# A hybrid recurrent and convolution encoder block: products on array quarters, first weights loaded earlier, a transform stage spread over tiles

## The chip, the cores and the metric

The kernel runs on one core of one Trainium2 chip. Its time is the device time of one execution in microseconds (us); the median of several runs is given. The profiled execution is a run of its own.

## The reference

One encoder block over 2048 tokens of 1024 channels, float32. The first half of the block, in which the change lies, computes this (RMSNorm, GeLU and the expert layer behind it are as usual):

```python
proj = rmsnorm(x) @ w_in                      # 1024 -> 2560: lru_x | lru_gate | v | x1 | x2, 512 each
xc = dwconv4(lru_x)                           # per direction d, heads of 64 channels:
r, i = sigmoid(xc @ wr + br), sigmoid(xc @ wi + bi)   # block diagonal, 8 blocks of 64 x 64
log_a = -8 * r * softplus(-lam);  a = exp(log_a)
h = scan(a, sqrt(1 - a * a) * (i * xc))       # forwards, and with other weights backwards
y_lru = (h_forward + h_backward) * gelu(lru_gate)
z = sin(f1 * (feats @ w1 + b1)); z = sin(f2 * (z @ w2 + b2))
filters = (z @ w3) * decay                    # 2 orders x 2 directions x 512 channels x 2048 positions
k = fft(filters / sum(abs(filters)))
y_hy = x2 * longconv(x1 * longconv(v, k1), k2)        # by FFT; v, x1, x2 through dwconv3 first
x = x + concat(rmsnorm(y_lru), rmsnorm(y_hy)) @ w_out
x = x + moe(rmsnorm(x))                       # top-1 of 4 groups, top-2 of 8 experts
```

## The kernel before

The program is a chain of stages. Within each, the five engines run programs of their own that are written out by hand and held together by semaphores; each engine and each queue works strictly in its written order. Between stages all engines meet, and SP clears the semaphores of the next one.

**Norm and filters** (`norm_and_filters`, L110). x is normalised and transposed. The filter network gives `zzd`, a pair of halves of 64 rows, the unused ones zero. The long filters are then made in 32 steps j (position j modulo 32). `generate` (L229) is one product for each of two orders o: stationary 128 x 128 out of `zzd`, moving `w3`, 512 channels. The stationary operand is block diagonal, forward filter and backward filter. VectorE multiplies the result by the decay (L374), ScalarE takes the magnitude (L303), GpSimd sums it (L200), `transform` (L243) is the first stage of the FFT of an earlier step, ScalarE empties its bank (L309) and SP stores it. On TensorE the order is generate(j), transform(j - 2). SP loads each decay tile (256 KB) four steps ahead. ScalarE and VectorE also split the normalised x into a high and a low part (L319, L355). At the end the sum goes through a product with ones (L255) and sixteen small ones (L259); with these the skip is scaled and added to filter row 0 (L379, L382), and the last transform follows.

**Projections** (`project_and_lru`, L396). The 2560 columns of `w_in` are 20 tiles of 128. A tile is 4 chunks of 512 tokens x 8 blocks of rows x 3 products of high and low parts, 96 passes (L521). SP loads its weights two tiles ahead (L457), ScalarE rounds them (L583), VectorE subtracts (L698). `TILES` gives the order: for each c of 0 to 3 the tiles v, x1, x2 of 128 channels (the last x2 after x of the RG-LRU), then x and g of the RG-LRU in turn. A tile of v, x1 or x2 is convolved by VectorE (L704, L706) and transposed (L543). For v the transposes go on into `spread` (L552), the first FFT stage of the signal: for each c 4 pieces of two products with 64 rows each, ScalarE empties them (L616) and stores them. `turn` does all four pieces at once, ahead of the transposes of the following x1 tile.

**RG-LRU**, inside the same stage, for each c: `gate` (L534) computes four gates (two kinds, two directions) of 4 chunks each, a block-diagonal 128 x 128 stationary operand made of two heads. ScalarE applies the sigmoids (L591). `decay` is Exp, Tanh and Sqrt (L634 to L637). VectorE: `weigh` (L725), `lru_input` (L729, L731), the scans (L735), `add_directions` (L739), the next convolution, the weight subtraction, and `gate_result` (L744). The gates of c + 1 may write T, the sigmoids' output, only when `gate_result` of c is done.

**Convolution** (`conv`, L798) is sent to the same engines behind the stage before. Of each block, `k_product` (L933) and `z_product` (L944) use column halves of the array and `inverse` (L957) row halves. GpSimd makes one difference per block (L1050), and for block 0 a one-row copy (L1054). VectorE runs the last backward scan, the last addition and the last gate product between the blocks 0, 3 and 6.

## Time and profile before

| | us |
|---|---|
| median of 3 runs | 2301.02 (2298.18 to 2305.28) |
| profiled execution | 2303.28 |
| its span | 2301.5 |
| TensorE busy | 2068.6 (90%) |
| VectorE busy | 1221.4 (53%) |
| ScalarE busy | 1115.4 (48%) |
| GpSimd busy | 345.9 (15%) |

The span runs from the first to the last instruction, and busy times are shares of it. PE is a product on TensorE, PEld a weight load, DVE is VectorE, ACT ScalarE, POOL GpSimd, SPq the queue of SP. A timeline row gives start, length, engine, line, operation, output and input by the program's names, how many instructions are merged, and in brackets the idle time ahead with what ended it. A merged row of products is as long as from the first start to the last end, and the ends of pipelined products overlap the next start. Every fp32 product appears as two passes; those of the projections (fp32r) as one.

### The profile page before, as it was taken

How to read it: one execution, taken by the hardware profiler on the slowest of the kernel's cores; microseconds unless marked ns; L12 is line 12 of the kernel's file. 1: busy time of each engine (PE TensorE's matmuls, PEld its weight loads, DVE VectorE, ACT ScalarE, POOL GpSimd, SP SyncE). 2: the span in 40 equal slices, each digit the busy share in tenths (PEclk: the TensorE clock that was granted, in tenths of full speed). 3: DMA queues.
4: the chain of work that ended last, by engine and by line, in shares of the span. 5: the costliest groups of instructions: out<-in, count | busy, mean ns of one | idle time of the engine just before them, and what ended most of it. 6: DMA issues, size and time to landing. Idle time of an engine off the chain costs nothing. (4 is left out here: it accounts for less than half of the span.)

```text
span 2301.5 us, 30650 instructions
## 1 busy us (share of the span) xinstructions
PE 2068.6 (90%) x9069; PEld 1500.0 (65%) x9070; DVE 1221.4 (53%) x1111; ACT 1115.4 (48%) x1315; POOL 345.9 (15%) x309
## 2 busy tenths in 40 slices
PE   3996999999999997878999669999999999999990
PEld 1654787786666421226878558888788788888870
DVE  7552322223666654663444475466868655664643
ACT  6762222225555532342333145466867765665643
POOL 0560000000000230220000011212111121221120
PEclk9997999999999999998999769999999999999995
DMA  5461213213111699757542356787999987886858
GB/s 190 157 226 62 64 55 92 73 37 94 39 38 38 244 341 348 273 192 249 178 165 96 128 193 196 249 275 252 374 310 375 374 293 222 297 284 207 291 145 313
DMA packets 239629, 462.08 MB, mean 201 GB/s; under 512 B 24897, under 2 KB 87461, under 8 KB 235174
## 3 DMA queue, kind: packets, MB, share of 16 engines
q1 hardware_dynamic: 201798, 375.17, 45.6%
q0 software_dynamic: 14400, 52.44, 9.5%
q10 hardware_dynamic: 23360, 33.56, 4.5%
q8 instruction: 42, 0.69, 0.1%
q14 instruction: 29, 0.23, 0.0%
HBM read 346.79 MB, written 114.29 MB: 200 GB/s over the span
## 5 line engine op out<-in xcount | busy, mean ns | idle before, releaser
L1762 PE MATMUL p<-wh_hi,x_hi 128*128 128x512 f32 x768 | 309.0, 402 | 1.7 <-DVE x_lo L1876 0.6
L1762 PE MATMUL p<-wh_hi,x_lo 128*128 128x512 f32 x768 | 304.4, 396 | 0.0
L1762 PE MATMUL p<-wh_lo,x_hi 128*128 128x512 f32 x768 | 304.2, 396 | 0.0
L1888 DVE TENSOR_TENSOR wh_lo<-w_raw,wh_hi 128x2048 fp32r<-128x2048 f32 x128 | 284.8, 2286 | 27.6 <-ACT wh_hi L1849 27.6
L521 PE MATMUL ps<-h_hi,wp_hi 128*128 128x512 f32 x640 | 257.7, 403 | 15.3 <-DVE wp_lo L698 15.3
L521 PE MATMUL ps<-h_lo,wp_hi 128*128 128x512 f32 x640 | 254.6, 398 | 0.0
L521 PE MATMUL ps<-h_hi,wp_lo 128*128 128x512 f32 x640 | 254.3, 397 | 0.0
L1849 ACT ACTIVATE wh_hi<-w_raw 128x2048 fp32r<-128x2048 f32 x128 | 234.8, 1924 | 0.4 <-DMA w_raw<-in_exp_w_dram 0.4
L1050 POOL TENSOR_TENSOR arena<-arena 128x512 f32<-128x512 f32 x32 | 56.9, 1778 | 762.4 <-DVE arena L1066 762.4
L1762 PEld LDWEIGHTS p<-wh_hi,x_hi 128*128 128x128 f32 x768 | 144.9, 189 | 35.6 <-issue 1.7
L1762 PEld LDWEIGHTS p<-wh_hi,x_lo 128*128 128x128 f32 x768 | 145.0, 189 | 35.2
L1762 PEld LDWEIGHTS p<-wh_lo,x_hi 128*128 128x128 f32 x768 | 145.0, 189 | 32.8
L1762 PE MATMUL pyy<-wy_hi,a_hi 128*128 x392 | 159.9, 408 | 5.9 <-ACT yb L1833 4.7
L1762 PE MATMUL pyy<-wy_hi,a_lo 128*128 x392 | 155.8, 398 | 0.0
L1762 PE MATMUL pyy<-wy_lo,a_hi 128*128 x392 | 155.6, 397 | 0.0
L521 PEld LDWEIGHTS ps<-h_hi,wp_hi 128*128 128x128 f32 x640 | 121.4, 190 | 46.5 <-DVE wp_lo L698 16.9
L1888 DVE TENSOR_TENSOR wy_lo<-w_raw,wy_hi 128x2048 fp32r<-128x2048 f32 x64 | 144.2, 2286 | 8.8 <-ACT wy_hi L1849 8.8
L1903 DVE TENSOR_TENSOR a<-p,s 128x512 f32<-128x512 f32 x48 | 33.2, 691 | 214.6 <-ACT s L1862 214.6
L521 PEld LDWEIGHTS ps<-h_lo,wp_hi 128*128 128x128 f32 x640 | 121.3, 190 | 29.5 <-issue 1.0
L521 PEld LDWEIGHTS ps<-h_hi,wp_lo 128*128 128x128 f32 x640 | 121.2, 189 | 29.5
L589 ACT ACTIVATE hraw<-ps 128x512 f32<-128x512 f32 x48 | 28.7, 599 | 221.0 <-PE ps L521 221.0
L1849 ACT ACTIVATE wy_hi<-w_raw 128x2048 fp32r<-128x2048 f32 x64 | 120.8, 1923 | 25.0 <-DMA w_raw<-in_exp_w_dram 21.5
(300 smaller groups left out, 3537.0 us busy)
## 6 DMA issues: line engine op xcount, KB each, us to landing
w_raw<-in_exp_w_dram SPq DMA_DIRECT2D x512, 256.0 KB, 5.9
w_raw<-in_exp_w_dram SPq DMA_DIRECT2D x128, 512.0 KB, 10.7
scratch_KA<-work SPq DMA_DIRECT2D x32, 512.0 KB, 3.0
scratch_SI<-arena SPq DMA_DIRECT2D x32, 512.0 KB, 3.4
kin<-scratch_KA SPq DMA_DIRECT2D x21, 512.0 KB, 6.1
arena<-scratch_SA SPq DMA_DIRECT2D x21, 512.0 KB, 5.1
wp_raw<-in_w_in_dram SPq DMA_DIRECT2D x20, 512.0 KB, 3.8
h_raw<-in_x_dram ACTq DMA_DIRECT2D x4, 2048.0 KB, 20.2
```

The costliest lines, as they stand in the source:

```text
L521: last = pe.matmul(out, w[:, s, k, :], h, start=(k == 0 and i == 0), stop=(k == KC - 1 and i == 2))
L589: ins = act.activation(out[:, 512 * n:512 * (n + 1)], pj[n], func)
L1050: dif = pool.tensor_tensor(yr[:, n % 2, :], by_r[:, n % 2, 0, :], by_i[:, n % 2, 1, :], ALU.subtract)
L1762: mm = pe.matmul(acc[:, :], x[:, k, :], w, start=(k == 0 and i == 0), stop=(k == n - 1 and i == 2))
L1849: act.activation(place, raw[:, j:j + 2, :], ACT.Copy).then_inc(rounded, 1)
L1888: dve.tensor_tensor(lo, raw[:, j:j + 2, :], hi.bitcast(F32), ALU.subtract).then_inc(lowered, 1)
L1903: dve.tensor_tensor(a[:, :], p3[:, :], s1[:, :], ALU.mult).then_inc(a_ready, 1)
```

## The change

`generate` and the gates of c = 1 to 3 no longer use one block-diagonal product of 128 rows and 128 columns but two of 64 x 64, each on its own quarter of the array, and the second order (or the backward direction) uses the two other quarters. So that one's results lie with their partition halves exchanged. The tables `fa_filter` and `decay` get a second, rolled copy for the second order (decay: 512 KB a step), `zzd` becomes `zz` of half the size. In the RG-LRU the backward direction of c = 1 to 3 lives in exchanged halves: GpSimd issues copies that exchange the parameters once, `xc` after each convolution (into the buffer of `xraw`), and the backward scan's result before the addition. `gate` of c = 0 stays.

The first two weight tiles are loaded by SP in the filter stage, behind the last `generate`, into the place of `zz`, and the loads at the start of the projections go. The skip waits for the norm product alone. `spread` is called for one piece behind each chunk of the projection of the tile after x1 (j = 2, 5, 8, 11), and ScalarE empties and stores it there. `gate_result` runs in four chunks, each waiting for its chunk of G; from c = 1 on, `add_directions` stands behind the next convolution and the weight subtraction. `early_loads` of the convolution waits for the last exchanged product instead of the last convolution.

```diff
@@ -118,21 +118,25 @@
     with ExitStack() as ctx:
         sb = lambda name, shape, dt=F32: ctx.enter_context(nc.sbuf_tensor(name, shape, dt))
         sem = PhaseSemaphores(nc, ctx)
+        marks["w_at"] = -(-nc.sbuf_base // 32) * 32
+        ka1, acc_flat = sb("ka1", [P, 2 * CH]), sb("acc", [P, 2 * CH])
+        marks["w_raw_at"] = -(-nc.sbuf_base // 32) * 32
+        zz = sb("zz", [P, SEQ])
+        w_first = nc.alloc_sbuf_tensor_at("w_first", [P, 2, KC, P], F32, offset=marks["w_raw_at"])
...
-        dec = sb("dec", [P, 4, CH])
-        ka1, acc_flat = sb("ka1", [P, 2 * CH]), sb("acc", [P, 2 * CH])
...
             for j in range(N2):
                 if j >= 4:
...
                 if j >= 5:
                     store(j - 5)
             sp.wait_ge(k_ready, N2 - 2)
-            sp.dma_start(skip, dram["hy_skip"]).then_inc(skip_in, 16)
+            for o in range(2):
+                sp.dma_start(skip[o], dram["hy_skip"][:, o, :]).then_inc(skip_in, 16)
+            sp.wait_ge(kgen, N2)
+            w_v = dram["w_in"].rearrange("o (k p) n -> p (o k) n", p=P)
+            for j, column in enumerate((1024, 1536)):
+                sp.dma_start(w_first[:, j], w_v[:, :, column:column + P]).then_inc(w_first_in, 16)
             for i in range(N2 - 5, N2):
                 store(i)
+            sp.wait_ge(w_first_in, 32)
             for s in range(3):
                 sp.wait_ge(kst_out[s], 16 * len(range(s, N2, 3)))
...
             pe.wait_ge(mlp_sin, 3)
-            view = zzd.rearrange("p h (q l) -> p l h q", l=N2)
+            view = zz.rearrange("p (q l) -> p l q", l=N2)
 
             def generate(j):
                 if j >= 2:
                     pe.wait_ge(k_ready, j - 1)
                 for o in range(2):
-                    last = pe.matmul(pk[j % 2][:, o, :], view[:, j], w3[:, o, :], start=True, stop=True)
+                    for h in range(2):
+                        rows, out = slice(R * h, R * h + R), slice(R * (h ^ o), R * (h ^ o) + R)
+                        last = pe.matmul(pk[j % 2][out, o, :], view[rows, j], w3[rows, o, :], start=True, stop=True)
...
 
             generate(0)
@@ -252,12 +265,13 @@
             pe.wait_ge(k_ready, N2)
             pe.wait_ge(summed, N2 + 2)
             for o in range(2):
-                pe.matmul(pk[0][:, o, :], ones[:, :], acc[:, o, :], start=True, stop=True)
+                last = pe.matmul(pk[0][:, o, :], ones[:, :], acc[:, o, :], start=True, stop=True)
+            last.then_inc(norm_mm, 1)
             for o in range(2):
                 for c in range(CT):
                     place = (o * CT + c) * 2
                     last = pe.matmul(pk[1][:, 0, place:place + 2], acc[:, o, c * P:(c + 1) * P], ones[:, 0:2], start=True, stop=True)
-            last.then_inc(norm_mm, 1)
+            last.then_inc(sums_mm, 1)
             transform(N2 - 1)
...
                     low_part(j // 2 - 2)
             dve.wait_ge(norm_mm, 1)
-            dve.wait_ge(skip_in, 16)
-            dve.scalar_tensor_tensor(out=skip, in0=pk[0][0:1, :, :], scalar=EPS, in1=skip, op0=ALU.add, op1=ALU.mult).then_inc(norm_ready, 1)
-            dve.wait_ge(norm_ready, 1)
+            dve.wait_ge(skip_in, 32)
+            for o in range(2):
+                dve.scalar_tensor_tensor(out=skip[o], in0=pk[0][R * o:R * o + 1, o, :], scalar=EPS, in1=skip[o], op0=ALU.add, op1=ALU.mult).then_inc(norm_ready, 1)
+            dve.wait_ge(norm_ready, 2)
             dve.wait_ge(abs_ready, 1)
-            dve.tensor_tensor(kt0[0:1, :, :], kt0[0:1, :, :], skip, ALU.add).then_inc(k0_ready, 1)
+            for o in range(2):
+                first = kt0[R * o:R * o + 1, o, :]
+                dve.tensor_tensor(first, first, skip[o], ALU.add).then_inc(k0_ready, 1)
             for i in range(NT - 2, NT):
                 low_part(i)
+            dve.wait_ge(sums_mm, 1)
...
         w_lo, w_raw = in_place(nc, ctx, "wp", [P, 2, KC, P])
+        raw_tile = lambda j: (marks["w_first"] if j < 2 else w_raw)[:, j % 2]
...
             rows = [("lru_conv_w", Q_CONV_W), ("lru_conv_b", Q_CONV_B), ("lru_br_f", 5), ("lru_bi_f", 6),
                     ("lru_br_b", 7), ("lru_bi_b", 8), ("lru_lambda_f", 9), ("lru_lambda_b", 10),
                     ("hy_conv_w", Q_HW), ("hy_conv_b", Q_HB), ("grp_norm_lru_g", Q_GA), ("grp_norm_hy_g", Q_GA + 1)]
@@ -506,6 +525,18 @@
             pool.memset(prow[:, :], 0.0)
             pool.memset(WG[:, :, :], 0.0).then_inc(zeroed, 1)
 
+            def exchange(out, a, done):
+                for h in range(2):
+                    pool.dma_start(out[halves[h]], a[halves[1 - h]]).then_inc(done, 16)
+
+            pool.wait_ge(lam_ready, 1)
+            exchange(PT_swapped, PT, pt_swapped)
+            for c in range(1, CT):
+                pool.wait_ge(xc_ready, c + 1)
+                exchange(xc_swapped, xc, xc_exchanged)
+                pool.wait_ge(scanned, 2 * c + 2)
+                exchange(I[1], T[1], exchanged)
+
...
+                    if j < 12 and j % 3 == 2:
+                        spread(j // 3, n)
                     if j == 0 and n == 0:
...
+            def gate_quarters(c):
+                pe.wait_ge(xc_ready, c + 1)
+                pe.wait_ge(wg_in, 16 * 8 * (c + 1))
+                for kind in range(2):
+                    for n in range(NCHUNK):
+                        u = kind * NCHUNK + n
+                        b = 2 * (u % 2)
+                        pe.wait_ge(evac, after(gate_place[c] + u // 2 - 1, b + 1))
+                        for d in range(2):
+                            for h in range(2):
+                                rows, out = halves[h], halves[h ^ d]
+                                last = pe.matmul(pj[b + d][out, :], WG[rows, 2 * d + kind, R * h:R * h + R], xc[rows, n * 512:(n + 1) * 512],
+                                                 start=True, stop=True)
+                            last.then_inc(mm_done, 1)
+
             def transposes(s):
 
...
-            def spread(c):
-
-                for b in range(4):
-                    pe.wait_ge(tr_evac, c * PER_C + SPREAD + (0 if b < 2 else 2 * b - 2))
-                    for g in range(2):
-                        h = slice(g * HALF, g * HALF + HALF)
-                        pe.matmul(tp[2 * b % 4 + g], fs[h, :], tst[h, 4 * b:4 * b + 4, :], start=True, stop=True).then_inc(tr_done, 1)
-
-            def turn(s):
-                if s % 3 == 1:
-                    spread(s // 3)
-                transposes(s)
+            def spread(c, b):
+
+                pe.wait_ge(tr_evac, c * PER_C + SPREAD + (0 if b < 2 else 2 * b - 2))
+                for g in range(2):
+                    h = slice(g * HALF, g * HALF + HALF)
+                    pe.matmul(tp[2 * b % 4 + g], fs[h, :], tst[h, 4 * b:4 * b + 4, :], start=True, stop=True).then_inc(tr_done, 1)
...
             def high(j):
-                act.wait_ge(w_in[j % 2], 16 * (j // 2) + 16)
-                act.activation(w_hi[:, j % 2], w_raw[:, j % 2], ACT.Copy).then_inc(w_high, 1)
+                at_least(act, w_in[j % 2], 16 * (j // 2))
+                act.activation(w_hi[:, j % 2], raw_tile(j), ACT.Copy).then_inc(w_high, 1)
...
-                    high(j + 1)
-                evacuate(f, out, func, chunks=range(2, 4))
+                for n in range(NCHUNK):
+                    if n == 2 and 1 <= j < len(TILES) - 1:
+                        high(j + 1)
+                    evacuate(f, out, func, chunks=range(n, n + 1))
+                    if j < 12 and j % 3 == 2:
+                        evacuate_spread(j // 3, n)
 
             def evacuate_turned(s):
-                if s % 3 == 1:
-                    act.wait_ge(tr_done, s // 3 * PER_C + SPREAD + 8)
-                else:
+                if s % 3 != 1:
...
+                act.wait_ge(tr_evac, first + 2 * b + 2)
+                act.dma_start(dram["SA"][0][:, 8 * b:8 * b + 8, c * P:c * P + P],
+                              spread_out[:, b % 2].rearrange("p l g n -> p (l g) n")).then_inc(sa_out[b % 2], 16)
 
             def decay(c, d):
-                act.wait_ge(evac, after(gate_place[c] + 2 * d))
+                act.wait_ge(evac, after(gate_place[c] + (1 if c else 2 * d)))
                 if d:
                     act.wait_ge(scanned, 2 * c + 1)
                 elif c:
                     act.wait_ge(y_out, 16 * c)
                 else:
...
+            def sigmoid_quarters(c):
+                for kind in range(2):
+                    for n in range(NCHUNK):
+                        u = kind * NCHUNK + n
+                        for d in range(2):
+                            bank = 2 * (u % 2) + d
+                            act.wait_ge(mm_done, after(gate_place[c] + u // 2, bank))
+                            act.activation((T, I)[kind][d][:, 512 * n:512 * (n + 1)], pj[bank], ACT.Sigmoid,
+                                           bias=col_of((Q_BR, Q_BI)[kind][d], c, d)).then_inc(evac, 1)
 
...
+                    if c == 1:
+                        act.wait_ge(pt_swapped, 32)
+                    sigmoid_quarters(c)
                 decay(c, 0)
...
-                    act.wait_ge(xc_ready, c + 1)
+                    if c:
+                        act.wait_ge(weighed, c)
+                    else:
...
             def weigh(c, d):
-                dve.wait_ge(evac, after(gate_place[c] + 2 * d + 1))
-                step(dve.tensor_tensor(I[d], I[d], xc, ALU.mult))
+                dve.wait_ge(evac, after(gate_place[c] + (3 if c else 2 * d + 1)))
+                if c and d:
+                    dve.wait_ge(xc_exchanged, 32 * c)
+                    dve.tensor_tensor(I[d], I[d], xc_swapped, ALU.mult).then_inc(weighed, 1)
+                    dve.wait_ge(weighed, c)
+                else:
+                    step(dve.tensor_tensor(I[d], I[d], xc, ALU.mult))
 
...
             def add_directions(c):
                 dve.wait_ge(scanned, 2 * c + 2)
-                step(dve.tensor_tensor(T[0], T[0], T[1], ALU.add))
+                if c:
+                    dve.wait_ge(exchanged, 32 * c)
+                step(dve.tensor_tensor(T[0], T[0], I[1] if c else T[1], ALU.add))
 
             def gate_result(c):
                 by_row = lambda a: a.rearrange("p (n q) -> p n q", n=HALF)
-                dve.wait_ge(evac, after(place["g", c]))
-                dve.tensor_tensor(Q.rearrange("p (q n) -> p n q", n=HALF), by_row(T[0]), by_row(G), ALU.mult).then_inc(y_ready, 1)
+                for n in range(NCHUNK):
+                    rows = slice(n * HALF // NCHUNK, (n + 1) * HALF // NCHUNK)
+                    dve.wait_ge(evac, after(place["g", c], n))
+                    last = dve.tensor_tensor(Q.rearrange("p (q n) -> p n q", n=HALF)[:, rows], by_row(T[0])[:, rows], by_row(G)[:, rows], ALU.mult)
+                last.then_inc(y_ready, 1)
 
...
                 lru_scan(1)
-                add_directions(c)
+                if c == 0:
+                    add_directions(c)
                 lru_conv(c + 1)
                 low(TILES.index(("g", c)) + 1)
+                if c:
+                    add_directions(c)
                 gate_result(c)
...
         def early_loads(sp):
-            sp.wait_ge(marks["xc_ready"], CT)
+            sp.wait_ge(marks["weighed"], CT - 1)
             sp.dma_start(kin[0], pair_rows("KA", 0)).then_inc(kin_in[0], 16)
...
-    out = dict(fa_filter=F, fa_signal=np.concatenate([F[:HALF], F[:HALF]]), inv_a=IA,
+    out = dict(fa_filter=np.stack([F, np.roll(F, HALF, 0)], 1), fa_signal=np.concatenate([F[:HALF], F[:HALF]]), inv_a=IA,
                fwd_b=full.reshape(N2, P, P).transpose(1, 0, 2), inv_b=inv.reshape(PAIRS, P, 2, P).transpose(1, 0, 2, 3),
-               feats=feats, decay=decay, ident=np.eye(P))
+               feats=feats, decay=np.stack([decay, np.roll(decay, HALF, 0)], 2), ident=np.eye(P))
     return {k: np.ascontiguousarray(v, dtype=f) for k, v in out.items()}
 
```

## Rows read from the trace of the kernel before

**Rows 1.** Busy time by stage: length, engines, TensorE clock, DMA share, GB/s.
```profile
74.40:175.70 101.30, 101.30 (x238) 57.26 (x237) 53.76 (x44) 72.33 (x75) 72.96 (x31) 1.00 0.66 219
204.30:549.80 345.50, 334.68 (x1489) 263.58 (x1490) 96.39 (x82) 83.18 (x142) 0.00 (x0) 0.98 0.23 65
549.80:769.80 220.00, 214.82 (x819) 151.92 (x820) 139.74 (x57) 137.89 (x145) 0.00 (x0) 1.00 0.15 41
```

**Rows 2.** Timeline of TensorE in the filter loop.
```profile
124.18 1.88 PE L229 MATMUL fk<-w,zzd 128*128 128x512 f32 x4
...
127.62 1.88 PE L229 MATMUL fk<-w,zzd 128*128 128x512 f32 x4
```

**Rows 3.** Timeline of TensorE in the convolution blocks, on array halves.
```profile
954.29 1.99 PE L957 MATMUL ps<-arena,inv_b 64*128 64x512 f32 x8
...
959.79 1.99 PE L957 MATMUL ps<-arena,inv_b 64*128 64x512 f32 x8
```

**Rows 4.** DMA queue in the filter loop (74.4 to 175.7): packets, MB, share.
```profile
q1 hardware_dynamic: 11668, 22.08, 66.2%
```

**Rows 5.** DMA queue at the convolution's start (770 to 800).
```profile
q1 hardware_dynamic: 3926, 11.31, 97.4%
```

**Rows 6.** Timeline of TensorE at the end of the filters.
```profile
180.90 1.84 PE L259 MATMUL fk<-ones,acc 128*128 128x2 f32 x16
```

**Rows 7.** Timeline of VectorE where the projection stage starts.
```profile
197.77 0.06 DVE L691 MEMSET xraw<- 128x2 f32 x1 [9.94 <-PEq L88]
```

**Rows 8.** Timeline of ScalarE, the same place.
```profile
201.98 1.06 ACT L583 ACTIVATE wp_hi<-wp_raw 128x1024 fp32r<-128x1024 f32 x1 [11.85 <-DMA wp_raw<-in_w_in_dram]
```

**Rows 9.** Timeline of TensorE: last passes of projection tiles 1, 2, 3, 8 and 9.
```profile
250.77 0.40 PE L521 MATMUL ps<-h_hi,wp_lo 128*128 128x512 f32 x1
...
274.97 0.40 PE L521 MATMUL ps<-h_hi,wp_lo 128*128 128x512 f32 x1
...
306.54 0.40 PE L521 MATMUL ps<-h_hi,wp_lo 128*128 128x512 f32 x1
...
434.91 0.40 PE L521 MATMUL ps<-h_hi,wp_lo 128*128 128x512 f32 x1
...
468.06 0.40 PE L521 MATMUL ps<-h_hi,wp_lo 128*128 128x512 f32 x1
```

**Rows 10.** Timeline of TensorE, gates of c = 1.
```profile
610.45 3.59 PE L534 MATMUL ps<-hc,WG 128*128 128x512 f32 x8
615.77 10.57 PE L534 MATMUL ps<-hc,WG 128*128 128x512 f32 x24 [1.72 <-ACT hraw L591]
```

**Rows 11.** Timeline of VectorE in the RG-LRU.
```profile
611.28 3.72 DVE L744 TENSOR_TENSOR tst<-hraw,spread 128x2048 f32<-128x2048 f32 x1 [0.72 <-ACT spread L589]
...
662.81 7.12 DVE L706 SCALAR_TENSOR_TENSOR hc<-xraw,PT,hc 128x2048 f32<-128x2048 f32 x3
```

**Rows 12.** Timeline of ScalarE, sigmoids of c = 1.
```profile
615.03 2.42 ACT L591 ACTIVATE hraw<-ps,PT 128x512 f32<-128x512 f32 x4 [2.19 <-DVE tst L744]
...
627.08 1.28 ACT L634 ACT_TABLE_LOAD   x1
```

**Rows 13.** Timeline of VectorE at the convolution's start: the last scan.
```profile
780.30 4.41 DVE L735 TENSOR_TENSOR_SCAN hraw<-tst,hc 128x2048 f32<-128x2048 f32 x1
```

**Rows 14.** Timeline of GpSimd, the same place.
```profile
778.33 1.77 POOL L1050 TENSOR_TENSOR arena<-arena 128x512 f32<-128x512 f32 x1 [579.97 <-DVE arena L1066]
780.16 4.95 POOL L1054 COPY arena<-arena 1x512 f32<-1x512 f32 x1
```

**Rows 15.** Timeline of TensorE, the same place.
```profile
786.31 2.94 PE L957 MATMUL ps<-arena,inv_b 64*128 64x512 f32 x8
```

**Rows 16.** Single lines of GpSimd: durations in ns, least, median, most.
```profile
L1054 POOL COPY arena<-arena x2: 687/2819/4951, 780.2 to 941.6; 1x512 f32<-1x512 f32 x2
...
L1715 POOL DMA_INDIRECT xg<-scratch_H,curidx x50: 993/1003/2869, 1349.4 to 2231.5; - x50
...
L1728 POOL DMA_INDIRECT scratch_X<-yb,curspot x50: 1586/1606/1623, 1368.1 to 2249.0; - x50
```

More of the change, by code:

```diff
@@ L134, in norm_and_filters @@
         ka, acc, kt0 = [kst[:, 3], split(ka1)], split(acc_flat), split(gain)
-        skip = dec[0:1, 0:2, :]
+        skip = [dec[R * o:R * o + 1, 0, o, :] for o in range(2)]
         pair = lambda name: ctx.enter_context(nc.psum_tensor(name, [P, 2, CH], F32))
@@ L242, in transform @@
                 for o in range(2):
-                    last = pe.matmul(pa[i % 2][:, o, :], fa[:, :], tile(j)[:, o, :], start=True, stop=True)
+                    last = pe.matmul(pa[i % 2][:, o, :], fa[:, o, :], tile(j)[:, o, :], start=True, stop=True)
                 last.then_inc(fa_done, 1)
@@ L441, in project_and_lru @@
         steps = sem("p_steps")
+        pt_swapped, xc_exchanged, weighed, exchanged = (sem(n, 0) for n in ("pt_swapped", "xc_exchanged", "weighed", "exchanged"))
+        halves = [slice(R * h, R * h + R) for h in range(2)]
         w_v = dram["w_in"].rearrange("o (k p) n -> p (o k) n", p=P)
@@ L573, in _ @@
                 if TILES[j] in GATED:
-                    for g in range(4):
-                        gate(GATED[TILES[j]], g)
+                    gate_quarters(GATED[TILES[j]])
         @block.scalar
```

75 lines of the change are left out of this document (33 added, 42 removed).

## The prediction, made before the changed kernel was run

> **What bounds the kernel now.** I read the page first, then the busy time by stage, then TensorE's timeline in each stage that the diff touches, and last what the other engines do where TensorE waits. The stages [rows 1] show TensorE busy for all 101.3 us of the filter loop, for 334.7 of the 345.5 us of the first twelve projections, and for 214.8 of the 220.0 us in which the RG-LRU follows. There the reader is to see that nothing else comes near: ScalarE has 72.3, 83.2 and 137.9 us in the same stretches. So in these stages a change is worth what it takes off TensorE's own sequence. What it takes off another engine is worth only what TensorE waits for that engine. The share of the copies is 0.66 in the filter loop, which matters below.
>
> **Filter loop.** One step is one `generate` (two fp32 products, each run as two passes over 512 columns) and one `transform` (the same). `generate` starts at 124.18 and again at 127.62 us [rows 2]: a step is 3.44 us, and its eight passes take 0.43 us each with no gap. The change splits each product of `generate` into two with 64 rows and 64 columns. That makes eight passes in place of four, on four quarters of the array. The trace before has no quarters. It has halves: in the convolution blocks [rows 3] eight passes on halves (x8) take 1.99 us or less, so two run at once, and a block of 24 passes that changes twice between row halves and column halves repeats every 5.50 us (954.29 to 959.79). Twelve slots of 0.43 us would be 5.16, so two changes of array shape cost 0.34 us. From these rows `generate` is bounded by 0.86 us (four quarters at once), 1.72 (two at once, as the halves) and 3.44 (one at a time). I take 0.86: halves by row and halves by column each overlap fully, and the four quarters of one `generate` are distinct in both. TensorE's step is then 1.72 + 0.86 + 0.34 = 2.92 us.
>
> The next limits, over the 29.5 steps of the stretch [rows 1]: ScalarE 72.33 / 29.5 = 2.45 us, GpSimd 2.47, VectorE 1.82, all below 2.92. The copies are not. The decay table is now loaded twice as wide, so a step moves 512 + 512 KB = 1.05 MB instead of 0.79. The filter loop moved 22.08 MB in 101.3 us at a share of 66.2% [rows 4], which is 329 GB/s for full engines: 3.19 us a step. The stretch with the heaviest traffic shows 11.31 MB in 30 us at 97.4% [rows 5], or 387 GB/s: 2.71 us. The new table has rows of twice the length, nearer to the second. Copies and TensorE compete for the bound and do not mesh perfectly, so I take 3.1 us a step. The saving is 0.34 x 29 = 9.9 us (bounds 2.93: 14.8; 3.44: none).
>
> The Trainium skill (TensorEngine Tiling (Array Packing), Restrictions and Gotchas) says that different row tiles cannot access the same PSUM bank simultaneously. Here the two row halves of one `generate` product do write one bank, on different partitions; the halves in this trace always wrote different banks, so no row bears on it. By the rule only two quarters could run at once, or fewer; these are the second and third rivals below.
>
> **Filter tail.** The VectorE step that adds the skip to filter row 0 now waits only for the four norm passes, not for the sixteen small products behind them, which take 1.84 us [rows 6]. Its two instructions become four of half the length; I charge 0.2 us for the extra starts. Saving 1.6 us (bounds 0.5 and 1.8). The three memsets taken from VectorE at the start hid behind the wait for parameters: nothing.
>
> **First weights.** VectorE enters the projection stage at 197.77 us [rows 7], ScalarE rounds the first weights at 201.98 after a wait for their copy [rows 8], and TensorE follows by rounding and subtracting. Loaded during the filters, they let ScalarE start at once: 4.2 us, less 0.2 for four more semaphores that are cleared in between: 4.0 (bounds 3 and 4.5). What is moved: two 512 KB copies are issued ahead of the last five filter stores on SP's queue, and the first waits for the last `generate`. Store 27 goes out some 3.5 us later, and ScalarE's evacuation 30 waits for it; only the last transform is behind that, which has to wait for the norm anyway. The parameter rows are now issued first by SP and gain 1 us.
>
> **Transform stage spread over projection tiles.** From the last pass of one projection to that of the next is 24.20 us without a spread (250.77 to 274.97), 31.57 with the first (274.97 to 306.54) and 33.15 with the third (434.91 to 468.06), which also met a slow clock [rows 9]; the second is like the first and the fourth like the third. The four cost 2 x 7.4 + 2 x 8.95 = 32.7 us. Of that 16 passes in pairs are 3.44 us each time; the rest is waiting for ScalarE to empty the banks and for stores to land. After the change one piece (four passes in pairs, 0.86 us, and two changes of shape, 0.34) stands behind each quarter of a projection, 5.6 us apart, while ScalarE has 5 us free. So 4 x 1.2 = 4.8 us for each c, and 0.5 for the transposes, whose third bank still waits for the last piece: 4 x 5.3 = 21.2 us. Saving 11.5 us (bounds 8, if every change of shape costs double, and 14). Nothing is idle long enough in it for the clock to fall.
>
> **RG-LRU gates, c = 1 to 3.** Now the first eight passes start at 610.45, TensorE waits 1.72 us for ScalarE, and 24 more start at 615.77 and take 10.0 us to the next projection [rows 10]: 15.3 us for each c. ScalarE starts its sigmoids at 615.03, when VectorE has done the gate product (611.28, 3.72 us) [rows 11, 12]. Three quarters of that product can now run before the last piece of G is there, but behind the weight rounding, which ends 0.72 us before 611.28 [rows 11]: it ends at about 614.4, 0.6 us sooner. (From c = 1 the addition of the directions stands ahead of it in place of ahead of the convolution, 2.3 us that only change places.) Then the first four sigmoids, whose banks are full, take 2.42 us [rows 12], 0.6 each, so a unit of quarters costs ScalarE 1.2 us and TensorE, from bank free to result, about 1.3 (0.86, one weight load, the drain). With four banks these alternate at about 1.28 us a unit. The next projection needs the first bank of unit 6: 8.7 us after the first sigmoid, against 10.7 now. Saving 0.6 + 2.0 = 2.6, three times 7.7 us (bounds 3 and 10). ScalarE's own chain, which now leaves the sigmoids 12.0 us after their start (627.08), gains about as much, so the next tile's banks are not late.
>
> Added: two exchange copies of 1 MB for each c between partition halves, issued by GpSimd, which is idle here; the copies' share in this stage is 0.15 [rows 1]. The first has 10 us of cover (it is needed after the sigmoids). The second is issued at the end of the backward scan and needed behind the next convolution, 7.1 us for its last three taps alone [rows 11], and one weight rounding: nothing, as long as it lands within that.
>
> **Start of the convolution.** Here a wait is added with something behind it. GpSimd's program is in order: its last exchange waits for the last backward scan (780.30 + 4.41 us [rows 13]), and behind it stands the first difference of the convolution, which ran before that scan, with its one-row copy ending at 785.1 [rows 14]. TensorE's first inverse product started at 786.31 [rows 15] and needs it. After: scan end 784.7, two copies issued (no row for this kind; bounds nothing and the 1.6 us of GpSimd's scatter; I take the gather's 1.0, being the plainer of the two [rows 16]), then 1.77 for the difference and, without the scan beside it, 0.69 for the copy (4.95 beside it; both in [rows 16]): 789.3. TensorE is 3.1 us late and has idled into the slow clock, another 1.2: a loss of 4.3 us (bounds 1.5 and 8). The products of the next blocks leave no slack to win it back.
>
> **Sum.** 9.9 + 1.6 + 4.0 + 11.5 + 7.7 - 4.3 = 30.4 us. The profiled execution took 2303.3 us (span 2301.5); it becomes 2272.9. The median of the runs, 2301.0, is 2.3 lower: 2271.
>
> **Rivals.**
> First, the filter loop is bound by its copies: at 329 GB/s or less with the doubled table, a step stays at 3.3 to 3.44 us. For it: at equal efficiency to now the step is already 3.19. Against: longer rows. The filter part falls to 0 to 4: about 2279.
> Second, two quarters at a time: `generate` keeps 1.72 us and gains two changes of shape, a step of 3.78, which loses 0.34 x 29 = 9.9 us where 9.9 was gained; the gates, at 1.72 + 0.45 a unit, win only the 0.6 and a little. Left: 1.6 + 4.0 + 11.5 + 1 - 4.3 - 9.9 = 3.9 us, 2297, no change that can be told.
> Third, the other side: quarters run one at a time, because two row tiles hold one bank. `generate` is 3.44 us and a step 5.50: 60 us lost in the filters. A unit of gates is 3.44, eight are 27.5 against 15.3: 37 lost. Less 12.8 from the rest: 2301 + 84 = 2385. The point from which it decides: the rest of the change saves 12.8 us, which 29 steps eat up when four quarter products cost 1.8 us, 0.45 each; all at once they cost 0.21, in pairs 0.43.
> Fourth, the second exchange lands late. For it: GpSimd's one-row copy was held to 4.95 us beside a scan, so issuing beside VectorE may be slow too. Against: 7.1 us and more of cover, and idle copy engines. Price: 1 to 3 us for c = 1 and 2, and a longer hold of GpSimd at the end: about 2277.
>
> **Chances.** Forecast 0.60; first 0.14; fourth 0.10; second 0.09; third 0.05; something unseen 0.02. What a measurement of this kernel can tell from no change is about 0.3%, 7 us. Faster 0.86, same 0.07, slower 0.07. The forecast's own bounds (sums of the likely ends of its parts) are 2260 to 2281; with the first and fourth rival, and a part of the second, the range is 2258 to 2289.
>
> **What would show it.** Right: `generate`'s eight passes start within 0.5 us of one another and the filter step is near 3.1 us with the copies' share above 0.9; ScalarE's first rounding directly behind the stage's start; a projection tile with pieces near 29 us from last pass to last pass; next projection 8.7 us after the first sigmoid; GpSimd's first difference after the last backward scan and the first inverse product some 3 us later in its stage. Wrong: a step of 3.8 or 5.5 us, a wait of the addition of directions for the exchange, or a wait of the projections for banks that ScalarE now empties later.

## The result and the profile after

The changed kernel takes 2273.43 us (median of 4 runs, 2272.07 to 2274.30) and the kernel before 2303.15 (4 runs, 2298.18 to 2306.78): a ratio of 0.9868, 95% interval 0.9848 to 0.9889, so 1.3% faster. Forecast were 2271 us with a range of 2258 to 2289. The profiled execution took 2273.04 us with a span of 2271.3 us, 30.2 less than before, and the sum had 30.4. The total is right to 0.2 us, but its terms are not: one gain was sized 4.1 us too small, one did not appear, and the loss came out twice as large and by another mechanism.

The stages again, cut at the same events as [rows 1]: filter loop, first projections, RG-LRU (the prediction calls the second stretch twelve projections; it holds thirteen tiles, the first x of the RG-LRU among them. Columns as there; PE is TensorE, the last three are clock, DMA share, GB/s):
```profile
72.90:163.60 90.70, 90.65 (x356) 30.95 (x356) 52.59 (x44) 74.01 (x77) 86.03 (x31) 1.00 0.92 326
187.10:520.90 333.80, 333.80 (x1490) 259.99 (x1491) 96.16 (x82) 82.83 (x142) 1.32 (x2) 0.99 0.24 67
520.90:732.40 211.50, 200.76 (x914) 139.55 (x914) 139.19 (x66) 135.51 (x145) 6.16 (x10) 0.98 0.26 68
```
TensorE fills the filter loop as before, and now the projections too, where [rows 1] left 10.8 us idle. In the third stage it has 10.7 us of idle time, where [rows 1] has 5.2.

TensorE's timeline in the filter loop (start, duration to the last end, engine, line, names, shapes, count), which answers to [rows 2]:
```profile
118.73 1.02 PE L256 MATMUL fp<-work,fa 128*128 128x512 f32 x2
119.68 1.16 PE L242 MATMUL fk<-w,zz 64*64 64x512 f32 x8
120.78 1.98 PE L256 MATMUL fp<-work,fa 128*128 128x512 f32 x4
122.69 0.73 PE L242 MATMUL fk<-w,zz 64*64 64x512 f32 x4
```
`generate` starts at 119.68 and again at 122.69, a step of 3.01 us. Its eight quarter passes are over, and the transform has begun, 1.10 us after the first began. Two at a time they alone would need 1.72. The first four start within 20 ns of one another, the other four 0.54 us later. So four quarters ran at once, although the two row halves of a product write one PSUM bank on different partitions. Here the rule that the prediction cites (the Trainium skill, TensorEngine Tiling (Array Packing), Restrictions and Gotchas) did not hold the passes back. The rivals built on it, 2297 and 2385 us, are out.

The start of the convolution, first TensorE's timeline (in brackets: idle time before, and what ended it), then GpSimd's. They answer to [rows 14, 15]:
```profile
745.80 1.94 PE L997 MATMUL ps<-kin,fwd_b 128*64 128x512 f32 x8 [2.22 <-DMA fwd_b<-in_fwd_b_dram]
750.36 1.99 PE L1021 MATMUL ps<-arena,inv_b 64*128 64x512 f32 x8 [2.62 <-POOL arena L1118]
752.28 1.94 PE L1008 MATMUL ps<-arena,fwd_b 128*64 128x512 f32 x8
760.25 3.68 PE L997 MATMUL ps<-xraw,fwd_b 128*64 128x512 f32 x8 [6.03 <-DMA xraw<-scratch_KA]
763.86 2.94 PE L1021 MATMUL ps<-arena,inv_b 64*128 64x512 f32 x8
```
```profile
746.88 1.01 POOL L530 DMA_DIRECT2D hc<-hraw  x2 [52.69 <-DVE hraw L791]
747.91 1.28 POOL L1114 TENSOR_TENSOR arena<-arena 128x512 f32<-128x512 f32 x1
749.26 0.96 POOL L1118 COPY arena<-arena 1x512 f32<-1x512 f32 x1
```
GpSimd does what was foreseen: last scan, two issues of 0.5 us each, difference, one-row copy, and TensorE waits 2.62 us for it. Nothing foresaw the second wait. After one more product TensorE stands 6.03 us for the kernel block of block 3, the fourth one, and its passes then run at a granted clock of 0.50 (3.68 us for eight, 1.94 at 1.00 before the wait). From 747 to 777 us the queues show this:
```profile
q1 hardware_dynamic: 3356, 8.23, 78.6%
q0 software_dynamic: 160, 1.05, 14.9%
...
hc<-hraw POOLq DMA_DIRECT2D x2, 512.0 KB, 9.7
```
The 1.05 MB of the exchange take 14.9% of the sixteen engines for 30 us, 4.5 us of all of them. Before the change the loads filled this stretch (785 to 815 us there) to 97.1%. The load that TensorE waits for was issued long before the exchange and landed 22.7 us later. SP's timeline has its issue:
```profile
737.53 0.47 SPq L915 DMA_DIRECT2D xraw<-scratch_KA  x1
```
While the exchange's packets move (750.6 to 756.8 us) the loads get only 0.47 MB through. In the 3.5 us behind them it is 1.18 MB. The queues from 750.6 to 756.8 us:
```profile
q0 software_dynamic: 158, 1.05, 71.9%
q1 hardware_dynamic: 244, 0.47, 32.1%
```
From the last projection pass to the third inverse product, behind which the blocks repeat every 5.50 us, were 29.2 us and are 38.5.

### The profile page after: what moved, and what is told of

Same layout as the page of the kernel before. It is cut to its first block and busy times, and to the rows that moved or that the text cites. A ratio compares the mean times of both kernels' runs of the same rounds, so it can differ in the third digit from the quotient of the medians.

```text
span 2271.3 us, 31131 instructions
## 1 busy us (share of the span) xinstructions
PE 2038.0 (90%) x9293; PEld 1451.9 (64%) x9294; DVE 1216.1 (54%) x1123; ACT 1113.4 (49%) x1315; POOL 363.0 (16%) x323
## 3 DMA queue, kind: packets, MB, share of 16 engines
q0 software_dynamic: 15424, 58.78, 10.9%
## 5 line engine op out<-in xcount | busy, mean ns | idle before, releaser
L552 PEld LDWEIGHTS ps<-h_hi,wp_lo 128*128 128x128 f32 x640 | 120.8, 189 | 29.3
L1789 POOL COPY curspot<-spot 128x1 int32 x50 | 44.1, 882 | 526.7 <-ACT yb L1897 526.7
```

What stands on the lines that cost most here:

```text
L552: last = pe.matmul(out, w[:, s, k, :], h, start=(k == 0 and i == 0), stop=(k == KC - 1 and i == 2))
L1789: pool.tensor_copy(cur_spot[:, :], spot[:, ds(B, 1)]).then_inc(spot_ready, 1)
```

## The experiments

All kernels below ran in three sets, five rounds each. The kernel before had medians of 2301.99, 2304.18 and 2303.62 us in them. "The stretch" is the one just named. Differences from the control compare medians, also between sets.

### First set: the exchange at the start of the convolution

**control**, the changed kernel itself. 

> The changed kernel again, beside the others. Expected: 2273 us, the ratio to the kernel before between 0.985 and 0.989, and the same 38.5 us from the last projection pass to the first steady block of the convolution.

 Measured: 2274.13 us, ratio 0.9875 [0.9857, 0.9894], stretch 38.5 us.

**c3_full**, whole array for c = 3 (the early loads of the convolution wait for the last convolution again, as before the change):
```
-  for c in range(1, CT):   # GpSimd's exchanges
+  for c in QUARTERS:       # (1, 2)
...
-  gate_quarters(GATED[TILES[j]])
+  if GATED[TILES[j]] in QUARTERS: gate_quarters(...)
+  else: for g in range(4): gate(..., g)
```


> Only c = 3 goes back to gate products on the whole array, so the last exchange (2 transfers, 1 MB) is gone and the last sum is a plain addition. Theory (the last exchange costs the convolution its start: GpSimd waits for the last scan before its first subtraction, and the transfer takes the engines that bring the first kernel blocks): the stretch from the last projection pass to the steady block, 38.5 us now and 29.2 before the change, falls to about 30, the gates of c = 3 grow by 2.1 us, in all 6 us less, 2267. Rival (that stretch is long since TensorE starts it at the lower clock after a longer idle time, and the loads are late of themselves): it stays at 36 or more, and the run is 2273 to 2276.

 Measured: 2270.06 us, ratio 0.9862 [0.9842, 0.9882], 4.1 less than the control, with 31.4 us for the stretch. The stage before it is 1.9 us longer (546.9 against 545.0 us from the first projection pass to the last). The wait for the same kernel block in TensorE's timeline:
```profile
757.05 2.52 PE L1003 MATMUL ps<-xraw,fwd_b 128*64 128x512 f32 x8 [2.64 <-DMA xraw<-scratch_KA]
```
It is 2.64 us, not 6.03. The theory holds in its main part and the rival falls: 7.1 of the 9.3 us are the exchange's. The same kernel run again (c3_again, below) has 29.8 us for the stretch, so up to 8.7.

The traces also settle which half of the exchange costs. Here the block's load was issued 5.9 us behind the last projection pass and landed 16.4 us later; in the changed kernel it was issued 5.7 us behind and took 22.7. TensorE reaches this product 22.4 us behind the last projection pass in this run, 28.4 in the changed kernel. Without the late load the changed kernel, its wait for GpSimd included, would have been ready for it at 754.2 us, which is 22.4 too. So the 2.62 us of GpSimd stand in the shadow of the load and cost nothing of their own. c3_again agrees. There another load made the first inverse product 1.9 us later than here (17.7 and 15.9 us behind the last projection pass), and the third comes 1.6 us earlier all the same, since TensorE waits 0.45 us for the block, not 2.64, and keeps its clock:
```profile
752.54 2.40 PE L1027 MATMUL ps<-arena,inv_b 64*128 64x512 f32 x8
...
757.25 1.94 PE L1003 MATMUL ps<-xraw,fwd_b 128*64 128x512 f32 x8 [0.45 <-DMA xraw<-scratch_KA]
```

**gates_full**, `QUARTERS = ()`, no exchange at all. 

> All gates on the whole array, no exchange at all; the filters, the first weights, the spread stage and the gate product by chunks stay as changed. Theory: the gates part of the change gains about 7.4 us in c = 1 to 3 and gives back about 8 at the start of the convolution, so this run is at 2273 within 2 us. Rival (the start of the convolution has nothing to do with the exchanges): the gates' 7.4 us are lost and nothing comes back, 2281.

 Measured: 2276.47 us, ratio 0.9884 [0.9863, 0.9904], stretch 29.3 us. That is 1.5 us outside the expected 2273 within 2 us (2.3 above the control), and 4.5 us below the rival's 2281. The stage before is 549.8 us long, 4.8 more than the control's, and 9.2 us come back in the stretch. At the end of the first round of blocks 6.7 of them are left (120.8 us from the last projection pass, 127.5 in the control), so there this kernel is 1.9 us ahead. Yet its span is 2.5 us longer (2274.7 against 2272.2). The stages behind, which the edit does not touch, differ by several us from run to run, and one pair of traces carries no statement of this size about the total.

**exch_sp1**, the last exchange on SyncE's queue behind block 1's loads; GpSimd no longer issues it, and the early loads stay as changed:
```
+  def last_exchange():
+      sp.wait_ge(scanned, 2 * CT)
+      for h in range(2): sp.dma_start(I[1][halves[h]], T[1][halves[1 - h]]).then_inc(exchanged_last, 16)
...
+  if n == 1: marks["last_exchange"]()
```


> The last exchange is issued by SyncE, behind the loads of block 1 of the convolution, instead of by GpSimd ahead of its subtractions. If GpSimd's order in its queue is what costs (its first subtraction stood 2.6 us behind the scan), about 2.6 us come back and the late loads stay: 2271. If the traffic of the exchange is what costs (the wait on the first kernel blocks, 6.0 us), it is now queued behind those blocks and 5 to 8 us come back: 2266 to 2268. If the addition at block 3 now waits for the transfer on VectorE, some of it is lost again there: 2270 or more with a wait at the addition.

 Measured: 2272.33 us, ratio 0.9868 [0.9846, 0.9889]. TensorE's waits from 733 to 850 us in the changed kernel and then in this one (line waited, releaser: us in total, times, longest):
```profile
PE ps L997 <- DMA xraw<-scratch_KA: 6.8, 2, 6.0
PE ps L997 <- DMA kin<-scratch_KA: 3.2, 1, 3.2
PE ps L1021 <- POOL arena L1118: 2.6, 1, 2.6
```
```profile
PE ps L1010 <- DMA kin<-scratch_KA: 5.1, 2, 3.2
PE ps L1010 <- DMA xraw<-scratch_KA: 3.1, 2, 2.5
```
The wait for GpSimd's copy is gone and the long wait is 2.5 us. But a later block (`kin`) now waits 1.9 us more. The stretch is 31.6 us, as in c3_full, so the place of the early loads is not what costs. The next inverse product comes 2.3 us later than in c3_full: part of the loss has moved. None of the three forecasts fits as it was written. The start came back as in the second, the total did not, and the addition does not wait for the transfer. The total can't be told from the control's (2267.53 to 2275.04 us in single runs).

### Second set: what bounds the filter loop now

**half_decay**, which does not load the second order's half of the decay table and uses the first for both:
```
-  sp.dma_start(dec[:, j % 4], dram["decay"][:, j])
+  sp.dma_start(dec[:, j % 4, 0], dram["decay"][:, j, 0])
```


> The filter loop loads 256 KB of decay factors a step, not 512 KB; the other half is read from the first again, so the second kernel's halves get each other's factors (wrong values, same work on every engine). Theory (TensorE sets the step of 3.00 us, the copies only run close to it): the step stays at 3.00 and the run at 2273 to 2274. Rival (the copies set it, with 0.93 of the 16 engines taken): the step falls towards 2.8, times 30, and the run to 2268 or less.

 Measured: 2274.13 us, ratio 0.9869 [0.9854, 0.9885], a step of 3.00 us.

**paired**:
```
-  for j in range(2, N2):
-      generate(j)
-      transform(j - 2)
+  for j in range(2, N2, 2):
+      generate(j)
+      generate(j + 1)
+      for i in range(max(j - 3, 0), j - 1): transform(i)
```


> In the filter loop TensorE generates two columns and then transforms two, so it changes between quarters and full array once in two steps. Theory (a step of 3.00 is 2.57 us of passes and 0.43 us of two changes of shape): it falls to 2.79, times 30 this is 6.3 us, 2268. Rival 1 (the copies are next, since 0.93 of the engines at 3.00 us leaves a floor of 2.79): between 2.8 and 2.95, 2 to 6 us. Rival 2 (the changes cost nothing, and the 0.43 us is something else, such as the first pass's own fill): the step stays at 3.00, 2273.

 Measured: 2273.75 us, ratio 0.9861 [0.9844, 0.9879]. Twelve pairs in a row take 72.5 us: 3.02 us a step.

**paired_half**, both edits. 

> Both edits: pairs, and 256 KB of decay factors a step (the second kernel's factors are wrong, the work is the same). If the copies hold the pairs back, this is faster than the pairs alone: step 2.79 and 2267 or less. If TensorE or another engine holds them back, it equals the pairs alone.

 Measured: 2274.08 us, ratio 0.9865 [0.9849, 0.9880]; 2.91 us a step.

The same 70 us of the loop in the changed kernel, half_decay, paired and paired_half (columns as in [rows 1]):
```profile
84.00:154.00 70.00, 70.00 (x285) 23.72 (x282) 41.75 (x35) 57.10 (x59) 66.33 (x24) 1.00 0.99 355
```
```profile
84.00:154.00 70.00, 70.00 (x285) 23.74 (x281) 41.75 (x35) 57.02 (x59) 66.33 (x24) 1.00 0.81 264
```
```profile
84.00:154.00 70.00, 68.51 (x281) 25.20 (x280) 48.56 (x35) 56.32 (x60) 65.71 (x26) 1.00 0.99 353
```
```profile
84.00:154.00 70.00, 70.00 (x290) 25.68 (x289) 66.60 (x37) 58.78 (x61) 66.19 (x25) 1.00 0.80 272
```
In the changed kernel TensorE is busy throughout and the copies are at 0.99. A share of 0.99 alone would name the copies. Taking a quarter of the traffic away (0.99 to 0.81) leaves the step at 3.00, so TensorE holds it. Giving TensorE less to do also leaves it, and then TensorE idles for 1.5 us and VectorE waits for the copies, in its list of waits:
```profile
DVE work L389 <- DMA dec<-in_decay_dram: 19.1, 19, 1.6
```
Both bounds lie at 3.0 us. Each edit alone gains nothing, and both together gain 0.09 us a step, 2.7 us in the loop; VectorE is then busy for 66.60 of 70 us, and what holds it at 2.91 I have not taken apart. The total does not show the 2.7 us. In the profiled run the end of the filters (from the last transform of the loop to the last of all) is 13.9 us long, 11.1 in the changed kernel and 12.7 in its control, and its products run at the lower clock. My expectation took the 0.93 of the whole loop for the copies' share. In these 70 us it is 0.99, and a floor of 2.97 would have followed.

**c3_paired**, paired and c3_full together. 

> The pairs of the filter loop, and c = 3's gates on the full array (no last exchange). The two savings are in different stages and should add: 4.1 us of c = 3 (2270.1 against 2274.1 in the first set) and what the pairs alone give, so 2264 if they give 6.

 Measured: 2266.61 us (2265.44 to 2269.38), ratio 0.9837 [0.9823, 0.9850]: the fastest version, with an interval wholly below the control's. The 2264 expected with 6 us from the pairs was missed.

### Third set: the other parts undone, and the exchange later

**spread_old**, the transform stage in one piece per c behind its tile, as before:
```
-                    if j < 12 and j % 3 == 2:
-                        spread(j // 3, n)
...
+            def turn(s):
+                if s % 3 == 1:
+                    spread(s // 3)
+                transposes(s)
```


> Only the transform stage goes back to one piece per c behind a projection tile. Theory (each c loses the idle time of TensorE between the spread passes, which the projection passes now fill): 11.9 us over the twelve projections, as between the two traces, so 2286 against the control's 2274. Rival (part of the 11.9 us is not this edit's: the projections start in another phase of the clock and of the loads): 5 to 8 us, 2279 to 2282.

 Measured: 2285.75 us, ratio 0.9927 [0.9914, 0.9939], 11.6 above the control. From the first projection pass to the last it takes 555.9 us against 545.0. The theory holds. (At the thirteenth tile 10.3 us of the 10.9 are there.)

**weights_old**, the first two weight tiles loaded in the projection stage. 

> Only the first two weight tiles are loaded at the start of the projection stage again, as before. Theory: the first projection then stands about 19 us behind the last transform of the filters and not 15.4, so 3.7 us later and 2278. Rival (the small transfers ahead of the projection, or the split of the weights on ScalarE and VectorE, hold the first pass anyway): under 1 us, 2274 to 2275.

 Measured: 2279.44 us, ratio 0.9893 [0.9880, 0.9906], 5.3 above the control. From the last transform to the first projection pass are 16.7 us against 12.9. ScalarE's first rounding in this kernel, then in the changed one, where [rows 8] has a wait of 11.85:
```profile
188.48 1.06 ACT L622 ACTIVATE wp_hi<-wp_raw 128x1024 fp32r<-128x1024 f32 x1 [12.23 <-DMA wp_raw<-in_w_in_dram]
```
```profile
184.63 2.00 ACT L625 ACTIVATE wp_hi<-w_first 128x1024 fp32r<-128x1024 f32 x2 [8.40 <-PEq L88]
```
The theory holds at 3.8 us; the other 1.5 us of the total no landmark shows. (The numbers of "19 and 15.4" in the expectation counted to another event; their difference is what was tested.)

**exch_sp3**, as exch_sp1 with `if n == 3`, the addition at block 5 and the gate product at block 7. 

> The last exchange is issued by SyncE behind the loads of block 3 of the convolution, its addition stands at block 5 and the last gate product at block 7. Theory (the start of the convolution is bound by transfers, so the megabyte costs its own 4.5 us of the 16 engines wherever it is put there): the first blocks are as early as without the exchange (31 us behind the last projection pass, not 38.5), about 4 us are lost over the next blocks, 2271 to 2272, as with the exchange behind block 1. Rival (it only had to leave the first loads alone): nothing is lost later, 2267 to 2268.

 Measured: 2270.48 us, ratio 0.9855 [0.9840, 0.9870]. The stretch is 31.6 us. From the last projection pass to the end of the first round of blocks (the first product behind it) are 122.1 us, 121.1 in exch_sp1, and 125.8 and 127.5 in the changed kernel and its control. The four traces without a last exchange have 116.8 (c3_again), 118.9 (c3_paired), 119.5 (c3_full) and 120.8 (gates_full), and the kernel before 118.5. So the start is free again, and 1.3 to 5.2 us are lost over the next blocks. That leans to the theory's 4, but the four differ by 4.0 among themselves. The total lies below the theory's 2271 to 2272 and above the rival's 2267 to 2268, and equals that of c3_full. Between the two the case stays open.

**c3_again**, c3_full once more. 

> The version with c = 3's gates on the full array once more, for a ratio from a second set: 0.986 as in the first (0.9862) if its true value is there; 0.984 or less would put it level with the version that also has the pairs (0.9837), and the pairs would be worth nothing in it.

 Measured: 2270.70 us, ratio 0.9861 [0.9845, 0.9878], as in the first set. The pairs add 3.5 to 4 us in company of c3_full and 0.4 alone. In c3_paired the first projection pass stands at 185.73 us, in the two runs of c3_full at 187.81 and 187.57. The traces show two parts. From the first `generate` to the norm product at the end of the filters are 96.3 us in paired and c3_paired and 97.7 to 97.8 in all kernels without pairs: the pairs are worth 1.4 us there, because GpSimd's sum is done that much earlier. The other part is the clock at that end. The norm product's four passes, in control and then in c3_paired:
```profile
166.88 3.65 PE L268 MATMUL fk<-acc,ones 128*128 128x512 f32 x4 [3.19 <-POOL acc L211]
```
```profile
165.52 1.96 PE L271 MATMUL fk<-acc,ones 128*128 128x512 f32 x4 [2.23 <-POOL acc L211]
```
The granted clock is 0.52 in the first and 1.00 in the second. In `paired` they take 3.60 us (0.51), in the changed kernel's first profile 1.96 (1.00). So 1.7 us come and go here without an edit, and one trace of each kernel does not tell how often.

## Why the prediction was right, and where its terms were off

**Filter loop: forecast 9.9 us, measured 14.0** (176.97 to 162.96 us for the last pass of its last transform). The mechanism was right, four quarters at once; it rests on the timeline, since no run put `generate` back. TensorE's step was estimated at 2.92 us and is 3.00, so what comes on top of the six slots of 0.43, two changes of shape among it, is 0.43 us and not 0.34. Of the 4.1 us too little, about 2.9 are the step (3.1 against 3.00, 29 times); the rest lies in the first and last steps, which the count of 29 leaves out. The step that failed is "Copies and TensorE compete for the bound and do not mesh perfectly, so I take 3.1". They do mesh: half_decay shows that copies at 0.99 do not lengthen TensorE's step at all. The copies' two estimates, 3.19 and 2.71 us, enclosed the truth (3.0), and the longer rows brought the loop to 355 GB/s at 0.99. The first rival, copies that hold the step at 3.3 or more, is out.

**Filter tail: forecast 1.6, measured nothing** (last transform of the loop to the last of all: 11.04 us before, 11.14 after, and 12.74 in the control, where the norm product ran at the lower clock). The shortened chain is there, but another end came late. TensorE's waits at the end of the filters, before and then after:
```profile
PE fk L255 <- POOL acc L200: 1.5, 1, 1.5
```
```profile
PE fk L268 <- POOL acc L211: 3.2, 1, 3.2
```
The norm product waits for GpSimd's sum of magnitudes. GpSimd is busy for 86.0 of the 90.7 us of the loop (73.0 of 101.3 before), and the faster the loop, the further it is behind at its end. The prediction read 2.47 us a step for GpSimd against 2.92 and dropped it. It now takes 2.85 (86.0 over 30.2 steps). The fuller copies are not the reason, for half_decay has the same 66.3 us of GpSimd in its 70 us at a share of 0.81. What the trace shows is that every second sum now takes 3.35 us beside 2.34 us of VectorE's work, the others 2.37; before nearly all took 2.36. What in it makes the difference stays open. This is a release that moved, and the question "what is late next" was not asked there.

**First weights: forecast 4.0, measured 3.4 between the traces and 3.8 by weights_old.** The mechanism is the one described: ScalarE starts with the stage.

**Spread: forecast 11.5, measured 11.9 between the traces and 10.3 by spread_old up to the same tile (11.6 on the total).** One piece moves the next projection pass from 0.23 to 1.39 us behind the last, so it costs 1.16, where 1.2 was charged. TensorE's timeline, line L599 the piece:
```profile
241.59 0.40 PE L552 MATMUL ps<-h_hi,wp_lo 128*128 128x512 f32 x1
241.92 1.13 PE L599 MATMUL ps<-tst,fs 64*128 64x512 f32 x4
242.98 0.50 PE L552 MATMUL ps<-h_hi,wp_hi 128*128 128x512 f32 x1
```

**Gates: forecast 7.7, measured 8.3** (RG-LRU stage 219.8 to 211.5 us). From the last pass of a projection to the next projection were 15.56 us each time; they are 12.34, 13.50 and 13.43. gates_full has 14.76, so the gate product by chunks is worth 0.8 (0.6 forecast) and the quarters 2.4, 1.3 and 1.3 (2.0 each). TensorE's timeline for c = 1 and c = 2, answering to [rows 10]:
```profile
581.30 1.95 PE L580 MATMUL ps<-hc,WG 64*64 64x512 f32 x16
586.25 2.25 PE L580 MATMUL ps<-hc,WG 64*64 64x512 f32 x16 [3.01 <-ACT hraw L687]
...
638.31 1.95 PE L580 MATMUL ps<-hc,WG 64*64 64x512 f32 x16
643.15 4.43 PE L580 MATMUL ps<-hc,WG 64*64 64x512 f32 x24 [2.89 <-ACT hraw L687]
```
The first sixteen passes are done in 1.95 us instead of 3.59 for eight, and TensorE then waits 3 us for the first sigmoid. For c = 2 it comes back at the lower clock. Clock, DMA share and GB/s end these lines, c = 1 first:
```profile
581.00:593.60 12.60, 8.99 (x67) 2.04 (x66) 3.90 (x5) 10.49 (x17) 0.49 (x1) 1.00 0.84 208
...
643.00:651.50 8.50, 7.64 (x49) 1.60 (x49) 0.00 (x0) 7.30 (x13) 0.00 (x0) 0.80 0.43 123
```
That TensorE can come back from this wait at the lower clock was no part of the sum. Which c it hits changes: in c3_again the gaps are 14.20 us for c = 1 and 12.22 for c = 2. The gate product and the tile behind it (22.27 us, 22.57 before) made up for it. The fourth rival, a late second exchange for c = 1 and 2, did not show: no addition of directions waits for it in those stages.

**Start of the convolution: forecast -4.3, measured -9.3.** The wait argued from GpSimd's order is there, 2.62 us where 3.1 were forecast (the forecast's own terms add up to 789.2, not 789.3). But the first inverse product is only 1.6 us later in its stage (18.5 us behind the last projection pass, 16.9 before), and nothing of it is left two products on, where TensorE waits for the load of block 3 in any case. "The products of the next blocks leave no slack to win it back" was wrong: the 4.3 us were charged for a wait that costs nothing of its own. The step that failed stands before it, where the exchange copies are weighed: "idle copy engines", and a share of 0.15, are true of the RG-LRU stage for c = 1 and 2. The last exchange runs in the next stage, beside loads that fill the engines to 0.97 [rows 5], a row that the prediction itself used for the filter loop. There it made the load of block 3 land 6.0 us later (against c3_full), on the critical path. The whole 9.3 us are 6.6 by which that product starts later (28.4 us against 21.8 behind the last projection pass) and 2.7 of lower clock in the sixteen passes behind the wait. The term should have been priced from the traffic, at 1.05 MB over 387 GB/s, 2.7 us at least, in place of the 4.3; that it came to 6.0 no row of before would have told.

**The rest of the program** gained 2.0 us. They lie in the remaining blocks of the first round: at its end the loss is 7.3 us (125.8 against 118.5 us from the last projection pass; 9.0 in the control), and what stands behind takes 1413.7 us, 1413.6 before. So the errors, +4.1, -1.7, -0.6, +0.4, +0.6, -5.0 and +2.0, cancel to -0.2. The total was right partly by luck; the mechanisms of the large gains were right, the filter loop's by its timeline and the others by the experiments. The mechanism of the one loss was wrong.

## What to carry over

Price each added transfer in the stage in which it runs, not in the stage that its code belongs to, and ask which load is queued beside it: nothing waited for the same megabyte for c = 1 and 2, and at the start of the next stage it held back a load on the critical path by 6 us. For c = 3, leaving out the quarters or moving the exchange behind block 3 gains about 4 us. A wait that you foresee costs only what is left of it at the next wait behind it; look there before you charge it. A full DMA share beside a full TensorE does not say which one binds; halve the traffic alone, thin out TensorE's sequence alone, then do both. When a loop gets faster, look at the engine with the next highest busy time at the loop's end, since its lag is paid there.

## What the runs showed of the hardware

- Four 64x64 quarters ran at once, eight passes within 1.10 us, while two of them wrote one PSUM bank on different partitions.
- The filter step is 0.43 us longer than its six slots of 0.43 (3.00 us). Changing between quarters and full array and back is at most that: two `generate` in a row, with no change between them, start 0.98 us apart (paired), 0.12 more than two slots.
- The exchange of two times 512 KB between partition halves took 9.7 us to land beside loads and 4.5 us of all sixteen engines' time, 1.05 MB at 233 GB/s; loads alone ran at 387 [rows 5]. While its packets moved, the loads went at 76 GB/s (0.47 MB in 6.2 us).
- GpSimd's copy of one row of 512 took 0.96 us behind the scan and 4.95 us beside it (c3_full, where the scan runs from 745.61 us for 4.40; as [rows 14]):
```profile
745.46 4.95 POOL L1124 COPY arena<-arena 1x512 f32<-1x512 f32 x1
```
